# Two transformer blocks, the second with stick-breaking attention and an expert lookup: first half's scores moved into the projection, key scores next to their queries, top-k work space doubled

## The reference

```
def second_block(x, ...):
    for l in range(DEPTH):
        xn = rms_norm_2(x, norm1_g[l])
        x = x + mixing_sublayer(xn, w_in[l], ..., w_out[l])
        xn = rms_norm_2(x, norm2_g[l])
        x = x + peer_ffn(xn, peer_wq[l], peer_keys[l], peer_u[l], peer_v[l])

def stick_breaking_attention(q, k, v):     # 6 heads of 64, blocks of 128 queries
        z = einsum(q, k) * scale
        log_keep = where(before, -softplus(z), 0.0)
        log_keep_after = cumsum(log_keep, reverse) - log_keep
        w = where(before, exp(log_sigmoid(z) + log_keep_after), 0.0)
        out = w @ v

def peer_ffn(xn, wq, sub_keys, u_tab, v_tab):   # 8 heads, 128 + 128 keys, 16384 experts
    q = xn @ wq
    scores = einsum(q, sub_keys)
    sv, si = top_k(scores, 16)                  # of each side; then top_k of the 256 sums
    gate = softmax(best_s)
    act = einsum(x, u_tab[idx])
    y = einsum(gelu(act) * gate, v_tab[idx])
```

## Time and profile before

| | |
|---|---|
| median of 3 runs | 2533.54 us (2532.52 to 2538.37) |
| the profiled execution, its own time | 2545.09 us |
| its span, first to last instruction | 2543.3 us |
| busy: PE, DVE, ACT, POOL | 83%, 70%, 33%, 29% of the span |
| DMA moved | 700.63 MB, 536.90 of it by the gathers |
| mean granted TensorE clock | 0.922 of full speed |

### The profile page before, as it was taken

The page is one execution under the profiler, slowest core; times in us unless marked ns, Lnnn a source line. Parts: engine busy times, 40 slices in busy tenths (PEclk is TensorE's granted clock), DMA queues, the critical chain, the costliest instruction groups (busy, mean ns, idle before and its releaser), DMA issues. The chain is left out here.

```text
span 2543.3 us, 28227 instructions
## 1 busy us (share of the span) xinstructions
PE 2118.3 (83%) x8712; PEld 1372.6 (54%) x8712; DVE 1772.9 (70%) x4237; ACT 828.6 (33%) x2024; POOL 734.7 (29%) x679
## 2 busy tenths in 40 slices
PE   8689999689988976998888777789669988888777
PEld 6469987469978764544333322287545443333232
DVE  4767775757776635878787877575358687877775
ACT  4456654456655631211111111056312111111110
POOL 0220000310001233444444444212324444434442
PEclk9799999799998877999999999997779999999999
DMA  6144533124426506999999999755069999999996
GB/s 222 66 159 149 189 117 130 60 93 173 175 106 196 175 1 271 417 420 421 421 422 421 421 421 419 306 149 172 1 265 415 421 421 421 421 421 421 422 421 277
DMA packets 138668, 700.63 MB, mean 275 GB/s; under 512 B 14392, under 2 KB 38200, under 8 KB 66872
## 3 DMA queue, kind: packets, MB, share of 16 engines
q0 software_dynamic: 73728, 536.90, 50.9%
q1 hardware_dynamic: 64824, 162.35, 18.1%
HBM read 698.16 MB, written 1.05 MB: 275 GB/s over the span
## 5 line engine op out<-in xcount | busy, mean ns | idle before, releaser
L1868 PE MATMUL bank<-ARENA 128*128 128x512 f32 x2048 | 988.7, 630 | 231.5 <-DVE ARENA L2227 230.8
L1868 PEld LDWEIGHTS bank<-ARENA 128*128 128x128 f32 x2048 | 386.7, 198 | 810.9 <-DVE ARENA L2227 435.7
L2217 DVE CUSTOM_DVE_ANT_0 ARENA<-ARENA 128x1024 f32<-128x1024 f32 x512 | 625.9, 1223 | 238.3 <-DMA ARENA<-in_uv_rows,ARENA 230.3
L1682 POOL DMA_INDIRECT ARENA<-in_uv_rows,ARENA x512 | 569.4, 1112 | 747.1 <-PE bank L1868 664.4
L154 PE MATMUL bank<-PARTS,PARTS 128*128 128x256 f32 (+3 forms) x1488 | 488.9, 329 | 40.5 <-DVE PARTS L1240 16.1
L155 PE MATMUL bank<-PARTS,PARTS 128*128 128x256 f32 (+6 forms) x1552 | 502.3, 325 | 0.0
L156 PE MATMUL bank<-PARTS,PARTS 128*128 128x256 f32 (+6 forms) x1552 | 501.2, 324 | 0.0
L2011 ACT ACTIVATE ARENA<-ARENA 128x1 f32<-128x1 f32 x512 | 103.0, 203 | 1025.6 <-DVE ARENA L2217 1025.0
L154 PEld LDWEIGHTS bank<-PARTS,PARTS 128*128 128x128 f32 x1488 | 288.8, 194 | 67.6 <-DVE PARTS L1240 19.5
L155 PEld LDWEIGHTS bank<-PARTS,PARTS 128*128 128x128 f32 (+2 forms) x1552 | 302.4, 196 | 17.6
L156 PEld LDWEIGHTS bank<-PARTS,PARTS 128*128 128x128 f32 (+2 forms) x1552 | 301.7, 195 | 18.5
(11 more groups left out here) (262 smaller groups left out, 2035.6 us busy)
## 6 DMA issues: line engine op xcount, KB each, us to landing
ARENA<-in_w_up_tiles SPq DMA_DIRECT2D x44, 1024.0 KB, 5.6
ARENA<-in_w_down SPq DMA_DIRECT2D x44, 512.0 KB, 3.5
ARENA<-in_w_in SPq DMA_DIRECT2D x32, 512.0 KB, 7.4
ARENA<-in_w_out SPq DMA_DIRECT2D x32, 512.0 KB, 4.9
ARENA<-in_wq_tiles SPq DMA_DIRECT2D x16, 1024.0 KB, 10.8
ARENA<-in_w_in SPq DMA_DIRECT2D x40, 384.0 KB, 3.8
ARENA<-in_w_in SPq DMA_DIRECT2D x32, 256.0 KB, 3.0
ARENA<-in_uv_rows,ARENA POOLq DMA_INDIRECT x512, 21.7
```

Of the source, the lines that this page charges most:

```text
L1682: nc.gpsimd.indirect_dma_start(out=slot[i % SLOTS], out_offset=None, in_=table[:, :], in_offset=bass.IndirectOffsetOnAxis(ap=picked[:, t, ...
L1868: last = mm(row_banks[t][n][:, :], diag[i % N_DIAG], slot[i % SLOTS][:, D + n * 512:D + (n + 1) * 512], start=(c == 0), stop=(c == NPICK - ...
L2217: v.tensor_tensor_reduce(u, u, xn[:, t, :], 1.0, 0.0, ALU.mult, ALU.add, dots[:, t, c:c + 1]).then_inc(S("dots_ready"), 1)
```

## The change

In `mixing_in`, the stick-breaking work of groups 0 and 1 now stands between units of chunks 7, 8 and 9, and with it the mLSTM rows of both groups. The keys and queries are turned all at once in chunk 5. Six of the lows go to POOL. The masks leave POOL: `scaled` now subtracts a large number where a key is not before its query.

```
+                def of_pool(n):
+                    return n // KD in (4, 5, 6) and n % KD in (3, 7)
+
+                def lows(n):
+
+                    on_pool = sum(of_pool(i) for i in range(n))
+                    return n - on_pool, on_pool
...
+                def low_pool(pool, n):
+                    pool.wait_ge(S("in2_hi"), n + 1)
+                    nc.gpsimd.tensor_tensor(unit(n)[1], raw(n), unit(n)[0], ALU.subtract).then_inc(S("in2_lo_pool"), 1)
+
                 def low(dve, n):
+                    if of_pool(n):
+                        return
                     dve.wait_ge(S("in2_hi"), n + 1)
                     nc.vector.tensor_tensor(unit(n)[1], raw(n), unit(n)[0], ALU.subtract).then_inc(S("in2_lo"), 1)
...
+                        if 53 <= n < 59:
+                            sb_high(act, n - 53)
...
+                        if (c, k) == (8, 4):
+                            attend.magnitudes(act, 0, 1)
                         if (c, k) == (8, 5):
                             act.wait_ge(S("m_ready"), 1)
                             nc.scalar.activation(row(6), row(6), ACT.Exp, scale=-1.0).then_inc(S("em_ready"), 1)
                         if (c, k) == (8, 7):
                             act.wait_ge(S("ml_silu"), 1)
                             nc.scalar.copy(ml_hi, qkm).then_inc(S("ml_high"), 1)
+                        if (c, k) == (8, 6):
+                            attend.logs(act, 0, 1)
                         if (c, k) == (9, 6):
+                            attend.sb_weight(act, 0)
+                            attend.sb_weight(act, 1)
+                        if (c, k) == (9, 4):
                             act.wait_ge(S("in2_taken_dve"), 9)
                             act.drain()
                             nc.scalar.activation(og, og, ACT.Sigmoid)
...
                         if (c, k) == (7, 2):
-                            sb_low(dve, 2)
+
+                            for g in range(6):
+                                sb_low(dve, g)
...
+                            dve.drain()
+                        if (c, k) == (8, 2):
+                            attend.scaled(dve, 0)
+                            attend.scaled(dve, 1)
+                        if (c, k) == (9, 0):
+                            attend.softplus(dve, 0)
+                            attend.softplus(dve, 1)
+                        if (c, k) == (9, 2):
+                            attend.sb_arg(dve, 0)
+                            attend.sb_arg(dve, 1)
...
+                        if (c, k) == (5, 4):
+                            turn_sb()
+                        if (c, k) == (7, 2):
+                            attend.sb_scores(pe, 0)
+                        if (c, k) == (8, 3):
+                            attend.suffix_sums(pe, 0)
+                            attend.suffix_sums(pe, 1)
                         if (c, k) == (9, 2):
                             turn_cols()
+                        if (c, k) == (9, 4):
+                            attend.ml_rows(pe, 0)
+                    attend.ml_rows(pe, 1)
```

The moved functions are passed in as `attend`; their bodies are as before but for the mask:

```
+                        first = lambda x: view(x, (2 * P, len(heads)), (1, P))
+                        nc.vector.tensor_scalar(first(zs[j]), first(sb_bank[j]), HD ** -0.5, None, ALU.mult)
+                    nc.vector.scalar_tensor_tensor(last_blocks(zs[j], j), last_blocks(sb_bank[j], j), HD ** -0.5,
+                                                   const("strict_big", (0, len(heads)), (1, P)), ALU.mult, ALU.subtract
+                                                   ).then_inc(S("sb_scaled"), 1)
...
+                def magnitudes(act, *js):
+                    for j in js:
+                        act.wait_ge(S("sb_scaled"), j + 1)
+                        nc.scalar.activation(lg[j], zs[j], ACT.Abs)
+                    act.drain()
+                    for j in js:
+                        nc.scalar.activation(lg[j], lg[j], ACT.Exp, scale=-1.0)
+                    act.drain()
+
+                def logs(act, *js):
+                    for j in js:
+                        nc.scalar.activation(lg[j], lg[j], ACT.Ln, bias=1.0).then_inc(S("sb_log"), 1)
...
+                def suffix_sums(pe, j):
+                    t, heads = groups[j]
+                    n = len(heads) * P
+                    pe.wait_ge(S("sb_softplus"), j + 1)
+                    if t == 0:
+                        last = mm(sb_bank[j][:, 0:n], const("suffix"), lg[j], start=True, stop=True)
```

In `mixing_out`, banks are dealt anew, the lists are reordered, and the second half's adding, normalising and turning move into the row loop. The top-k work space exists twice: `choices[0]` for the two heads ahead of the loop and `choices[1]` for the others. The slots from the fourth on are dealt so that slots 4 to 7 lie over the first 512 columns' weights. On POOL:

```
-                        nc.gpsimd.tensor_tensor(x_rstd[:, t:t + 1], x_rstd[:, t:t + 1], HALF[:, 0:1], ALU.pow
+                        pool.wait_ge(S("x_sums"), t + 1)
+                        nc.gpsimd.tensor_tensor(x_rstd[:, t:t + 1], xss[:, 2 * t:2 * t + 1], HALF[:, 0:1], ALU.pow
                                                 ).then_inc(S("x_rstd"), 1)
...
+                    for n in range(N_LOW_DVE, 16):
...
                         if i == 4:
-                            x_root(1)
+                            pool.wait_ge(S("out2_done"), 2 * NT - 1)
+                        if i == 8:
                             pool.wait_ge(S("out2_done"), 2 * NT)
                         if i % TOPK == 0:
...
+                        if i == SLOTS + SUM_ROW - 3:
+                            x_root(1)
```

The work space, the `steps` and the places in the loop (- before, + after):

```
+            choices = [choice(WQ_AT + 7 * D, XN_AT + 3 * 512), choice(WORK_AT, WORK_AT + 1008)]
...
-            steps = [(0, (0,)), (1, (0,)), (2, (0, 1)), (0, (1,)), (3, (0, 1)), (1, (1,))] + [(h, (0, 1)) for h in range(4, PH)]
+            steps = ([(h, (0,)) for h in range(3)] + [(3, (0, 1))] + [(h, (1,)) for h in range(3)]
+                     + [(h, (0, 1)) for h in range(4, PH)])
             step_of = {(t, h): i for i, (h, ts) in enumerate(steps) for t in ts}
-            step_after_row = {1: 2, 9: 3, 17: 4, 25: 5, 33: 6, 49: 7, 65: 8, 81: 9}
+            step_after_row = {1: 2, 17: 3, 21: 4, 25: 5, 29: 6, 33: 7, 49: 8, 65: 9, 81: 10}
...
+            ADD_ROW, SUM_ROW, NORM_ROW, TURN_ROW, TAKE_ROW = 4, 6, 9, 9, 13
```

PE's list, its part from the scores of group 2 on:

```
+                    sb_scores(pe, 2)
+                    ml_rows(pe, 2)
+                    ml_rows(pe, 3)
                     turn_y(0)
+                    suffix_sums(pe, 2)
+                    suffix_sums(pe, 3)
                     out(0, 0)
-                    suffix_sums(2)
-                    suffix_sums(3)
+                    out(0, 1)
+                    sb_scores(pe, 4)
                     ml_scores(2)
-                    out(0, 1)
+                    ml_rows(pe, 4)
+                    turn_x(0)
+                    suffix_sums(pe, 4)
+                    queries(0)
+                    ml_scores(4)
+                    key_scores(0)
                     ml_values(2)
                     ml_values(3)
                     sb_values(2)
                     sb_values(3)
-                    sb_scores(4)
-                    ml_rows(4)
-                    turn_x(0)
-                    ml_scores(4)
-                    queries(0)
-                    suffix_sums(4)
                     ml_values(4)
                     sb_values(4)
+                    queries(1)
+                    key_scores(1)
                     turn_y(1)
-                    key_scores(0)
                     out(1, 0)
                     out(1, 1)
-                    queries(1)
-                    key_scores(1)
-                    turn_x(1)
```

DVE's list, its end:

```
-                    sb_arg(4)
+                    first_choice(0)
                     y_sums(1)
+                    second_choice(0)
                     y_scaled(1)
+                    numbers(0)
                     y_low(1)
-                    first_choice(0)
-                    second_choice(0)
-                    numbers(0)
-                    add_mixed(1)
-                    normed(1)
                     first_choice(1)
                     second_choice(1)
-                    take_x(1)
                     numbers(1)
                     for i in range(len(rows)):
                         row_dots(i)
                         if i >= 1:
                             diagonal(i - 1)
+                        if i == ADD_ROW:
+                            add_mixed(1)
+                        if i == SUM_ROW:
+                            x_sum(1)
+                        if i == NORM_ROW:
+                            normed(1)
+                        if i == TAKE_ROW:
+                            take_x(1)
```

More of the change, by code:

```diff
@@ new lines, in softplus, with sb_arg @@
+                def softplus(dve, j):
+                    dve.wait_ge(S("sb_log"), j + 1)
+                    nc.vector.scalar_tensor_tensor(lg[j], zs[j], 0.0, lg[j], ALU.max, ALU.add).then_inc(S("sb_softplus"), 1)
+                def sb_arg(dve, j):
+                    t, heads = groups[j]
+                    dve.wait_ge(S("sb_suffix"), j + 1)
+                    sums = view(sb_bank[j][:, 0:1], (P, len(heads)), (len(heads) * P, t + 1), (1, P))
```

(12 more changed lines are left out.)

503 lines of the change are left out of this document (220 added, 283 removed).

## The result

The changed kernel takes 2505.34 us (median of 4 runs, 2501.92 to 2505.89), the kernel before 2535.71 (4 runs, 2532.52 to 2538.37): a ratio of 0.9869 with a 95% interval of 0.9851 to 0.9887. It is faster, by 1.3%. The forecast was 2488, the range 2464 to 2512. The profiled execution took 2505.54 us, its span is 2503.8.

The account below looks back on a forecast made before the run. The prediction took DMA's gathers in the row loops as the bound. Its terms summed to -22.5 us per layer, -45 for two: 2545.09 to 2500, less 11.5 for the median, 2488.5; range 2464 to 2512.

Parts of the forecast that it names:

- Term A: Projection: grows by 20 us per layer from PE's added work, its wait for softplus and half clock; bounds +10 and +30.
- term B: Second part's start to the first half's mixed output: 65.1 us falls to 33, -32 per layer.
- I keep that difference: Final step: the runs' median lies 11.5 us under the profiled execution, so 2500 becomes 2488.5.
- Term C: First half's mixed output to first gather: 44.5 us falls to 39.7, -5 per layer; bounds -8 and -2.
- D and E: Stream of gathers: DMA's standstill after four gathers goes, -4.5 us; the later loss goes too, -1, per layer.
- Rival 3: PE falls to 1.2 GHz at its new standstill until the row loop: whole gain lost, or slower, 2554 us; chance 0.05.
- Rivals 1, 2 and 4: Suffix-sum wait hidden, 2468 us (0.17); waits cost more, 2516 (0.13); no change, PE can't use earlier rows (0.03).

Follow-up runs that it names:

- before_again: The kernel before, unchanged, run for a second profile: 2535.56 us.
- suffix_late: As softplus_first, also PE's suffix sums after unit 72 instead of 67 and ACT's cast of 128x1536 two units later: 2483.86 us.
- softplus_first: The changed kernel with DVE's two softplus one unit earlier, ahead of the low of unit 72: 2488.73 us.
- lows_on_dve: The changed kernel with all 80 lows on DVE, none on POOL: 2498.93 us.
- choices_late: The changed kernel with head 0's key scores behind the turning of y, its choices and numbers behind y's lows, head 1's queries behind the output: 2533.44 us.
- drain_back: The changed kernel with a drain of POOL ahead of each power of x_root: 2515.46 us.
- before_no_drain: The kernel before with the adding of the two sums of squares on DVE and no drain ahead of POOL's power: 2522.24 us.
- undo_front: The changed kernel with the first half's stick-breaking work and mLSTM rows of groups 0 and 1 back at the second part's start: 2485.96 us.
- undo_dve: undo_front and lows_on_dve together, against the changed kernel: 2490.52 us.

## Why the forecast came out right in direction and 17 us low

Per layer, against before_again, whose two layers agree: projection +21.2, to the mixed output -21.8, to the first gather -8.2, the stream -5.1. That is -13.9, two layers -27.8. The 30.0 us between the two spans hold another 2.3 ahead of block 2, where the code is the same; that is chance and no gain of the change. The text had +20, -32, -5, -5.5: -22.5.

**Term A was right** in sum and in its two large parts: wait 11.6 (10), PE's work 10.1 (10.3), +21.2 (+20). Its two small parts did not show and had cancelled each other by luck: PE's waits for lows stayed at 8.5 us against 8.6, where 2 us of gain were taken, and PE's growth of 10.1 holds the units at half clock, for which 2 were added. The wait was where it was said and named DVE. It comes from PE's place in the order (suffix_late); 5.5 us of it are DVE's low of unit 72 ahead of the softplus and the slowness of both beside POOL (softplus_first). The Trainium skill ("SBUF — State Buffer", section "SBUF: two separate sides") says that the port pair that VectorE (with two SBUF inputs) and GpSimd share goes to whichever starts first, for its whole instruction. The trace agrees: the low of unit 72 ends 0.42 us behind POOL's subtraction, about the time of a low alone. It agrees on the six lows too, which give nothing and cost 2.5 us of projection in both layers together (lows_on_dve); there A was 22, by the rule, and 21.2 measured.

**The step that failed is the base of term B**: "layer two is the example (layer one holds the same code)". The 65.1 us of the earlier trace rows belong to layer two of that execution, in which the 73 matmuls ahead of the turning of y ran at half clock throughout. The same part took 59.1 in layer one of the same trace, and 58.4 in layer two of the next execution. That is 6.5 us a layer. The new length was mis-sized too, 37 instead of 33. Half of that lies ahead of the turning of y, 20.8 us instead of 18.8. The other half lies behind it, 16.2 us instead of 14.2: the text took 4.7 us off its 18.9 for an output at full clock; the output did run at full clock, and 2.7 came of it. The sum before that deduction, 37.7, was the better one. The bounds, -35 and -27, miss the -21.8.

**"I keep that difference" belongs to the same error.** The 11.5 us by which the profiled execution lay over the median were taken off at the end as if the changed kernel would have them too; its profiled execution equals its median within 0.2. Most of that excess lay in the rows from which the sum was made, so layer two's excess was taken off both in B and at the end, and layer one, which had none, was given it in B. Counted from the median, that is the 6.5 us a layer above, 13 of the 17, and not a further error. The mis-sized length adds 8, A and the stream 3, and C takes 6 back.

**Term C** was -8.2 instead of -5, just over its bound: the sums came at 25.4 us, near the 24.7 that the text had for full clock, and the first gather at 37.4 where it had 37.1 for that case and took 39.7. choices_late shows that the part hangs on the order of the choices. **D and E** were right, -5.1 against -5.5, by the mechanism that was named for D: the power behind the drain comes only when the gathers in flight have landed (drain_back, before_no_drain). E went with the drain as well, in the kernel before too.

**The rivals.** Rival 3 was nearer than its 0.05 tells: PE did run at 1.2 GHz from the barrier on, though for 20 us and not until the row loop. What it cost there lies between 5 us a layer (37.0 against 32.3, which still has 10 us at half clock) and 12, an estimate from 25.2 us of PE's work that leaves out all waits. And the move in front, which the kernel seemed to be about, was a loss of 19 us (undo_front), outweighed by the reordered choices, the missing drain and the other edits of the second part. Rivals 1, 2 and 4 did not come: the wait was full; PE's waits for lows did not grow; and DMA stays at 0.98 to 1.03 from 5 us behind the first gather to 60, so the rows were used as fast as they came.

## What to carry to other kernels

Before a part of the program is taken as the example, read the same part in every layer: where they differ with the same code, the number is one of the execution. And when the profiled execution is longer than the median, look for the excess in the rows that the sum uses. Work that is moved to another part pays only if its operands are made before PE's place in the list is reached: here PE stood 11.6 us for them, and five units later, with the softplus made one unit earlier, it did not stand at all (suffix_late). A drain on GpSimd with gathers in flight held it until they had landed (8.3 and 18.5 us here), so let another engine make the operand that the drain guards.

## What the runs showed of the hardware that was not expected

TensorE was granted 0.50 of its clock (1.2 GHz) for 20 us in which it was busy 5.00 of every 5 us, with matmuls of 64 to 128 columns, right behind 15 us at 1.00 in which it was busy for 14.53; the same list of instructions took 37.0, 35.4 or 32.3 us in different executions and kernels, with 24, 21 or 10 us of it at half clock ((1 - clock) x 2 x length). The Trainium skill ("TensorE: Matmul & The Clock Gate", section "Part 1: The HAM clock gate (the "warmup" mystery)") has the clock follow how busy the array has been. Here a PE that the profile shows busy throughout ran at the lower level, in the changed kernel and in 15.5 us of the kernel before; no run settles why.

A drain on POOL stood 18.5 us behind sixteen gathers (drain_back), and 8.3 behind four.

Executions of one kernel lay within 14 us for the kernel before (2532.12 to 2546.34 over all runs), within 17 for undo_dve and within 3 for suffix_late.
